# First mixer: the context's queries projected between the attention pairs of x, with the pairs put in another order

## The reference

```
def mix_window_diff(h, hc, w_in, w_out, ..., rope):          # h: x, hc: context, 256 x 1024 each
    aq, bq, ak, av, bk, bv = split_cols(h @ w_in, AB_SPLITS)
    ak_c, av_c, bk_c, bv_c = split_cols(hc @ w_in[:, AB_Q_WIDTH:], AB_SPLITS[2:])
    aq, ak = rope(rms_norm(aq, ...)), rope(rms_norm(ak, ...)); ak_c = rms_norm(ak_c, ...)
    y_a = windowed_sink_attention(aq, ak, av, ak_c, av_c, a_sink)        # 8 heads of 64
    y_b = diff_attend(bq, [bk_c, bk], [bv_c, bv], lam)                   # 4 pairs: (p0 - lam*p1) @ v
    y_b = rms_norm(y_b, b_sub_norm) * (1.0 - lam_init)
    y = concatenate([y_a, y_b]) @ w_out
    aq_c, bq_c = split_cols(hc @ w_in[:, :AB_Q_WIDTH], AB_SPLITS[:2])    # the context's queries
    aq_c, bq_c = rms_norm(aq_c, ...), rms_norm(bq_c, ...)
    y_a_c = gqa_attend(aq_c, [(ak_c, av_c, None)], a_sink)
    y_b_c = rms_norm(diff_attend(bq_c, bk_c, bv_c, lam), b_sub_norm) * (1.0 - lam_init)
    y_c = concatenate([y_a_c, y_b_c]) @ w_out
```

## Time and profile before

| what | us |
|---|---|
| median of 3 runs (2531.42 to 2537.38) | 2532.72 |
| the profiled execution, its time | 2535.41 |
| its span | 2533.6 |
| PE busy, of the span | 2459.0 (97%) |
| DVE busy | 1613.0 (64%) |
| ACT busy | 1034.1 (41%) |

### The profile page before, as it was taken

How to read it: one execution, slowest core, us unless ns; L and a number is a source line. 1 busy time by engine, 2 the same in 40 slices (tenths; PEclk the granted TensorE clock), 3 DMA queues, 4 the chain that set the end, 5 groups by cost and what they waited for, 6 DMA issues and landing times. The chain is left out here.

```text
span 2533.6 us, 37324 instructions
## 1 busy us (share of the span) xinstructions
PE 2459.0 (97%) x15326; PEld 2150.3 (85%) x15326; DVE 1613.0 (64%) x2662; ACT 1034.1 (41%) x1676; POOL 0.2 (0%) x4
## 2 busy tenths in 40 slices
PE   8999899899999999999899999999999998999999
PEld 7998799899988888886678888888888887879999
DVE  6768544756677667568768767548555447846553
ACT  5545554445432222256533322224222226744442
POOL 0000000000000000000000000000000000000000
PEclk9999999999999999999999999999999999999999
DMA  8644534455545555353014555435555426502654
GB/s 281 205 157 132 178 117 125 156 178 167 176 157 176 168 163 166 109 174 117 1 42 154 169 164 171 133 92 172 165 175 167 128 92 171 187 9 73 183 183 146
DMA packets 143659, 372.23 MB, mean 147 GB/s; under 512 B 22378, under 2 KB 40450, under 8 KB 143490
## 3 DMA queue, kind: packets, MB, share of 16 engines
q1 hardware_dynamic: 143202, 369.54, 46.6%
q10 hardware_dynamic: 288, 0.31, 0.0%
HBM read 368.64 MB, written 1.15 MB: 146 GB/s over the span
## 5 line engine op out<-in xcount | busy, mean ns | idle before, releaser
L356 PE MATMUL psum<-normed_hi,weights_hi 128*128 128x256 f32 (+2 forms) x2664 | 879.7, 330 | 19.1 <-ACT arena L487 4.2
L356 PE MATMUL psum<-normed_lo,weights_hi 128*128 128x256 f32 (+2 forms) x2664 | 865.2, 325 | 0.0
L356 PE MATMUL psum<-normed_hi,weights_lo 128*128 128x256 f32 (+2 forms) x2664 | 864.2, 324 | 0.0
L304 DVE TENSOR_TENSOR weights_lo<-weights_raw,weights_hi 128x1024 fp32r<-128x1024 f32 (+2 forms) x547 | 657.7, 1211 | 259.8 <-ACT weights_hi L298 257.3
L298 ACT CAST weights_hi<-weights_raw 128x1024 fp32r<-128x1024 f32 (+2 forms) x547 | 562.5, 1036 | 314.3 <-DMA weights_raw<-in_w_down 197.3
L356 PEld LDWEIGHTS psum<-normed_hi,weights_hi 128*128 128x128 f32 (+1 forms) x2664 | 507.7, 191 | 79.9 <-issue 19.7
L356 PEld LDWEIGHTS psum<-normed_hi,weights_lo 128*128 128x128 f32 (+1 forms) x2664 | 508.1, 191 | 40.7
L356 PEld LDWEIGHTS psum<-normed_lo,weights_hi 128*128 128x128 f32 (+1 forms) x2664 | 508.5, 191 | 38.6
L975 DVE SCALAR_TENSOR_TENSOR arena<-arena,cond 128x512 f32<-128x512 f32 x392 | 273.0, 747 | 7.9 <-DMA arena<-in_w_mod 3.8
L356 PE MATMUL psum<-hidden_hi,weights_hi 128*128 128x512 f32 (+1 forms) x594 | 219.4, 369 | 0.0
L356 PE MATMUL psum<-hidden_lo,weights_hi 128*128 128x512 f32 (+1 forms) x594 | 217.4, 366 | 0.0
(11 more groups left out here) (273 smaller groups left out, 2820.2 us busy)
## 6 DMA issues: line engine op xcount, KB each, us to landing
weights_raw<-in_w_gu SPq DMA_DIRECT2D x220, 512.0 KB, 3.5
arena<-in_w_mod SPq DMA_DIRECT2D x256, 256.0 KB, 3.0
weights_raw<-in_w_down SPq DMA_DIRECT2D x110, 512.0 KB, 3.5
weights_raw<-in_w_x SPq DMA_DIRECT2D x24, 512.0 KB, 7.1
weights_raw<-in_w_qk SPq DMA_DIRECT2D x24, 512.0 KB, 3.5
weights_raw<-in_w_z SPq DMA_DIRECT2D x16, 512.0 KB, 3.6
weights_raw<-in_w_g SPq DMA_DIRECT2D x16, 512.0 KB, 3.5
weights_raw<-in_w_ssm_branch SPq DMA_DIRECT2D x16, 512.0 KB, 3.5
```

Source lines behind the costliest of these rows:

```text
L304: ve.tensor_tensor(w_lo[:, c % RING, a], w_raw[:, c % RING, a], w_hi[:, c % RING, a].bitcast(F32), ALU.subtract).then_inc(lo_ready, 1)
L356: last = te.matmul(out, a, b, start=start and n == 0, stop=stop and n == 2)
```

## The change

The eight steps of the context's query projection leave the first list. They are put behind the attention's steps 0 to 7 (`LinearBeside`: bank 5, and bank 7, which it shares with the turns; turns 8 and 9 lie between its first and second half). The eight differences of x (both tiles) come first, then the eight sinks of x, then the 16 pairs of the context as before. The norms and rotations of x's sink queries lie at steps 0 to 3 of the attention, those of the context's queries at steps 5 to 11, their turns at 12 to 14. Head norms of the keys and of the first queries of x are placed nearer to their projections: two side steps may follow one base step, and the norm's three steps follow one another. The idle matmuls of `keep_busy` in this attention go. The order of the turned outputs changes with the pairs. No computation is added or taken away.

```
+        class LinearBeside(LinearT):
+
+
+
+            beside_banks = (5, 7)
+            second_bank_free = ()
+
+            def bank(self, g):
+                return self.beside_banks[g % 2]
+
+            def wait_bank(self, pe, g):
+                if g >= 2:
+                    pe.wait_ge(*bank_free[self.group + g - 2])
+                if g % 2 == 1:
+                    pe.wait_ge(*self.second_bank_free[g // 2])
 
...
+                    for event in u.turn_needs:
+                        pe.wait_ge(*event)
                     if j >= 1:
...
-        heads = HeadNorms(head_items, head_space)
+        head_pairs = [HeadNorms(head_items[n:n + 2], head_space) for n in range(0, len(head_items), 2)]
...
-        h_steps, t_steps = steps_of(heads), steps_of(turns)
-        side = [(10 + j, h_steps[j]) for j in range(4)]
-        side += [(14, h_steps[4]), (15, h_steps[5])] + [(16, s) for s in t_steps[0:3]]
-        side += [(20, h_steps[6]), (20, h_steps[7])]
-        side += [(24, h_steps[8]), (24, h_steps[9])] + [(25, s) for s in t_steps[3:6]]
-        side += [(28, h_steps[10]), (28, h_steps[11]), (30, h_steps[12]), (30, h_steps[13])]
-        side += [(32, s) for s in t_steps[6:10]]
+        turn_items[8].needs.append(last_of(c_q, 1))
+        c_q.second_bank_free = (turns.done(7), turns.done(9))
+        h_steps, t_steps = [steps_of(pair) for pair in head_pairs], steps_of(turns)
+        side = []
+        for pair, first_place in ((0, 6), (1, 10), (2, 14), (3, 20), (4, 24)):
+            side += [(first_place + n, step) for n, step in enumerate(h_steps[pair])]
+        side += [*zip((11, 12, 14, 18, 19, 24), t_steps[0:6])]
+        side.sort(key=lambda placed: placed[0])
...
-                            *joined(down, norms, beside(steps_of(*ab_main), side))], (sums, 1)))
...
+                            *joined(down, norms, beside(steps_of(*ab_main[:-1]), side, per=2)), *t_steps[6:8]],
+                           (sums, 1)))
+
+        units = difference_pairs(0, [last_of(x_q, n) for n in range(1, 4)] + [turns.done(7)]) + difference_pairs(1, [])
+        units += sink_pairs(0, [turns.done(9)], [last_of(c_q, n) for n in (2, 3)]) + sink_pairs(1, [])
+        for t in (2, 3):
+            units += difference_pairs(t, [turns.done(13)] if t == NT else []) + sink_pairs(t, [])
+        attend = Attend(units, s_ab, turned_ab)
...
-        side = [(3 + n, step) for n, step in enumerate(h_steps[14:18])]
-        side += [(7 + n // 2, step) for n, step in enumerate(t_steps[10:14])]
-        for t in range(TT):
+        o_steps, q_steps = steps_of(out_turns), steps_of(c_q)
+        side = [*zip((0, 1, 2, 3, 4, 5, 6, 7), q_steps), *zip((0, 1, 2, 3), h_steps[5]), *zip((3, 3), t_steps[8:10]),
+                *zip((5, 6, 7, 8), h_steps[6]), *zip((8, 9, 10, 11), h_steps[7]), *zip((12, 12, 13, 14), t_steps[10:14])]
+        side += [(9, (subs[0], 0)), (10, (subs[0], 1)), (11, (subs[1], 0)), (15, (subs[1], 1))]
+        side += [*zip((16, 17, 18, 19), o_steps[0:4])]
+        for t in (2, 3):
...
-        in_order(beside(steps_of(attend), side, per=2))
+        side.sort(key=lambda placed: placed[0])
+        in_order(beside(steps_of(attend), side, per=3))
```

81 lines of the change are left out of this document (39 added, 42 removed).

## The result

The changed kernel took 2546.44 us, median of four runs (2544.91 to 2549.31), against 2533.94 (2531.42 to 2537.38) for the kernel before on the same chip: the ratio is 1.0046, with a 95% interval of 1.0033 to 1.0059. That is 12.5 us slower; forecast were 12.0, and 2544.7 us. The profiled execution took 2545.47 us, its span is 2543.7.

What follows compares the result with a forecast made beforehand. TensorE, busy 97%, was taken as the bound, with VectorE nearly as full around the moved projection. +13.3 up to the context, +0.5 after, -1.8 for clock gave +12.0: 2532.7 + 12.0 = 2544.7 us, range 2531 to 2552.

Steps and rivals of the forecast that it cites:

- Part 1, the front: Up to the first scores: new waits at turns 3 and 6, +1.0 us, first scores at 1161.9 us.
- Part 2, turn 8: Attention steps 0 to 3 with chunks 0 to 3: 28.8 us, TensorE standing 9 us ahead of turn 8.
- Part 3: Steps 4 to 7 with chunks 4 to 7: 26.6 us, VectorE and ScalarE setting the pace.
- that rival: Projection chunks wait for bank 7, so TensorE is not filled; its chance part of the slow-clock rival's 0.18.
- Part 4: Steps 8 to 15: 40.0 us to the context's first scores at 1257.3 us, 13.3 late, with a hole at turns 10 and 11.
- The clock term: Slow-clock phases of 0.9 (first scores), 1.7 (turn 8), 1.6 us (scores 13); 1.8 taken off for any not coming.
- the walk: Forecast method for the stage: following each engine's work list with durations from the earlier profile.
- its signs: Profile marks to confirm the forecast, including context scores about 103 us after x's query projection, against 90 before.
- Part 5: The context's pairs: two more output turns, one norm of differences gone; +0.5 us, from -0.5 to +1.1.
- Full overlap: Rival over steps 0 to 15: VectorE never waits for casts or scores, context 11.2 us early, total 2522; chance 0.13.
- half overlap: Rival: turn 8 costs 2 us instead of 9 and the splits' waits halve; +2 to +3, 2535; chance 0.21.
- The rival of a low clock through steps 8 to 12: TensorE at the lower clock there too: +18 us, total 2550; chance 0.18.

Runs made afterwards that it cites:

- e8: Changed kernel with ScalarE's casts of the coming weight chunks ahead of the step's exponentials (at step 4, swapped with turn 9's copy); median 2544.4 us.
- e2: Changed kernel with the head norms of attention steps 0 to 7 ahead of the same step's projection chunk; median 1 to 2 us under the changed kernel's.
- the first execution: First profiled execution of the changed kernel, with no further edit; 2545.47 us.
- the second: Profiled execution when the changed kernel was measured once more, unaltered; that measurement gave 2547.4 us, its stage 154.6 us.
- e3: Changed kernel with 12 idle matmuls ahead of turn 6 and 28 ahead of turn 8, which began late; turn 8 at 33.6 us instead of 29.2, total not given.
- e9: Changed kernel with idle matmuls: 12 ahead of turn 6, 30 from the start of turn 8's wait, 14 at step 12 by mistake; total not given.
- e5: Changed kernel with the context's query projection back in front of the attention; new pair order kept, idle matmuls still out; 2538.1 us.
- e7: e5 with turns 10 to 13 at steps 9 to 12 and sub norms at steps 12 to 15; median 2534.9 us.
- e10: e7 with idle matmuls: 6 and 8 at steps 2 and 4, 6 each at steps 8 and 16; 2532.8 us, ratio 0.9988 to the kernel before.
- e1: Changed kernel with turns 8 and 9 and chunk 4 behind the scores of attention step 4; turn 8 still at 29.2 us, total not given.
- e4: Changed kernel with x's sub norms moved to steps 12 to 15 and turns 10 to 13 one per step there; no gain in the median.
- e6: e2 plus the sub norms of e4, turns 10 to 13 left where they were; runs from 2541.4 to 2557.5 us.
- e11: Changed kernel with e2, e8 and e9 together, but 10 idle matmuls ahead of turn 8 and the 14 at step 11; 2545.1 us.

## Why the prediction was right, step by step

- **Part 1, the front: right.** Turn 3 waited 0.65 us (taken: 1.0), turn 6 3.5 (3.8), and the first scores came 6.8 us after x's queries (6.6). That they came at 1161.53 (1161.9) by the span's clock is partly luck: in other executions of the same front they come up to 6 us later. One sum is off: by its own rows a chunk is 2.86 us (1171.26 to 1173.89 and 0.23), not 2.74. A chunk without a turn ahead of it takes 2.74 in the trace, so little hangs on it.
- **Part 2, turn 8: right.** It came 29.2 us after the first scores (28.8), with 9.1 us of wait (9). Its cause as forecast, the chain from maxima over exponentials and cast to the split, was shown by e8, which cuts it on ACT and moves turn 8 by 3.2 us, and by e2. The forecast wait of 0.9 for each split was 1.25 in the mean, 2.4 for the first.
- **Part 3: right.** The maxima of pair 8 came at 1217.34 (1217.3; the steps named add up to 17.0 and not to the 17.2 used). No chunk waited for bank 7, so that rival did not occur. In the changed kernel the fifth chunk stood behind turn 9 at 1195.5, 4.8 us after turn 8 (5.4).
- **Part 4, right in the mechanism and 1.9 short in the first execution.** The context's scores came at 1259.19 (1257.3). The hole was foreseen at turns 10 and 11, as one of before's kind; in the trace it is the 4.1 us of wait at step 11, for a second copy behind sub norms on DVE, and turn 11 waits only 0.8. Scores 13 came 28.2 us after the maxima of pair 8 (26.0), the context's 13.7 after those (14.0). The clock term, 1.6 for this hole, was too small for this execution (17 us low). In the second (7 us low) the context came 100.3 us after x's queries, 1.7 earlier than the walk, which has 102.0 (the 103 among its signs is counted from before's mark).
- **Part 5: right in the first execution.** The context's pairs up to the output projection took 52.65 us against 52.48, 0.2 more (0.5). In the second they took 54.3, 1.9 more and outside the range of -0.5 to +1.1.
- **The clock is the term that was mis-sized.** I had 4.2 us for three phases and took 1.8 of these off, for phases that might not come. All three came, but no run shows the 0.9, 1.7 and 1.6 us that I put them at. The runs show in their place how long each lasted, 7, 7 and 17 us at a granted 0.50 in the first execution of the changed kernel, and what the first was worth: with the wait ahead of it filled, the first scores took 1.13 us and not 2.08 and pair 3 came 2.2 us earlier after them (e3, e9). Of the 14.5 us in the stage 8.5 are PE's longer waits, and PE is busy 6.0 longer though 14 idle matmuls of 0.24 us, 3.3 in all (e9's 30 took 6.86, 0.23 each), are gone from its list: 9.3 us through the clock. Much of that lay beside a slow DVE, which the walk had already, as e9 shows for the steps up to 8; the rest of it makes the stage longer than forecast. By the sums over the windows 13.7 us more are missing to the full clock (18.8 against 5.1), nearly the whole difference of the stage. PE's busy time shows 9.3 of it, and e9 took 10 us of the lower clock away for 1.5, as part of that time lay beside DVE's work or in waits.
- **The agreement of the sum is partly luck.** Forecast were 12.0 us, and the medians differ by 12.5. By the profiles, the stage and what stands ahead of it took 15.4 us more in the first execution and the stage 12.0 in the second, so single executions scatter by more than the forecast is off.
- **The rivals.** Full overlap (2522) and half overlap (2535) did not come: the splits waited 10 us, 1.25 each and not 0.2, and PE was busy 82.9 of the 104.5 us up to the context, 79% and not over 90%. The rival of a low clock through steps 8 to 12 (2550) was half there: the first execution had 17 us of it, from step 11 on instead of from step 8.

What stays open: why the same wait was followed by 7 us of lower clock in one execution and 17 in another; no run here separates that. Of the 5.9 us that e5 loses in the attention it isn't shown how much is the order of pairs and how much the side work at steps 9 to 15; e7, which spreads that work, is 8.1 us quicker up to the context, which speaks for the side work. How often the fall at step 16 of e7 comes isn't known: how much of e10's gain over e7 is the clock rests on the medians, 2532.8 and 2534.9, from different chips. And no edit of the kernel with the projection beside won back more than 2 to 3 us in the median, so that e5 shows the projection's place to be the cause, but only part of the 9.3 us is led back to a single wait.

## What to carry to other kernels

Before work of the fullest engine is moved beside a stage, list what the move brings onto the others: here each chunk of matmuls brought a cast and a split that had to pass the chain of maxima and exponentials, and DVE, busy 72.5 of 90 us, had no room. A wait that another engine's work sets was only moved by reordering the waiting engine's list (e1, e4, e6, e11); it got shorter where the engine that is waited for did something else in its own waits (e2, e8: turn 8 at 25.5 and 26.0 us instead of 29.2). Idle matmuls paid where TensorE was the pace setter and the wait behind which its clock fell was short (e10, in one execution: a granted 1.00 over 21 us where e7, with its wait of 1.9 us, had 0.51), and nearly nothing where it wasn't (e9: 1.5 us for 10 to 14 us less of the lower clock).

## What the runs showed of the hardware that was not expected

- A wait of 1.9 us in an otherwise busy TensorE was followed by 20 us at half clock (e7, granted 0.51), longer than around the wait of 9.1 us at turn 8 of the changed kernel (7 us). Within such a stretch TensorE was busy 20.56 of 20.60 us. In the changed kernel it was busy 17.19 of 18.00.
- Twelve idle matmuls in the wait of 3.5 us ahead of turn 6 kept the scores behind it at 1.13 us for four (e3, e9, e11) where the changed kernel had 2.08. After 30 of them, and 2.5 us of wait more, the clock still fell for 3 us (e9).
- The same program differs from run to run with the clock: e6 took 2541.4 us at a mean clock of 0.990 and 2557.5 at 0.980.
